# Latent attention's queries and keys turned by VectorE over device memory, with all such transfers issued by GpSimd

## The reference

```python
h = _rmsnorm(x, ln_g[l])
u = h @ w_in[l]                       # 2048 x 6232
y_a = _gla(...) * silu(g_a)           # gated linear attention
y_b = _ssd_mixer(...)                 # state space mixer
y_c = _mla(...) * silu(g_c)           # latent attention
y_d = _dilated_attention(...) * silu(g_d)
x = x + concatenate([y_a, y_b, y_c, y_d]) @ w_out[l]
```

```python
q = (_rmsnorm(c_q, q_norm_g) @ w_uq).reshape(Bsz, S, MLA_H, MLA_QK)
k = _rmsnorm(concatenate([k_nope, k_r]), k_head_g)
q = _rmsnorm(q, q_head_g)
q = concatenate([q[..., :128], _rope(q[..., 128:], positions)])
k = concatenate([k[..., :128], _rope(k[..., 128:], positions)])
return _causal_attention(q, k, v)
```

## Time and profile before

| | us |
|---|---|
| median of 3 runs | 814.8 (814.75 to 814.91) |
| the profiled execution, whole | 815.04 |
| its span, first to last instruction | 813.2 |
| TensorE busy | 806.8 (99%) |
| VectorE busy | 613.7 (75%) |
| ScalarE busy | 473.7 (58%) |
| GpSimd busy | 60.1 (7%) |
| SyncE's queue, share of the 16 transfer engines | 63.9% |

### The profile page before, as it was taken

The page is one execution under the profiler, slowest core; times in us unless marked ns, Lnnn a source line. Parts: engine busy times, 40 slices in busy tenths (PEclk is TensorE's granted clock), DMA queues, the critical chain, the costliest instruction groups (busy, mean ns, idle before and its releaser), DMA issues.

```text
span 813.2 us, 11261 instructions
## 1 busy us (share of the span) xinstructions
PE 806.8 (99%) x4164; PEld 684.3 (84%) x4164; DVE 613.7 (75%) x1092; ACT 473.7 (58%) x784; POOL 60.1 (7%) x64
## 2 busy tenths in 40 slices
PE   8999999999999999999999999999999999999998
PEld 5888887999887888888888888889998888888886
DVE  6678899877898766678964967979779977665452
ACT  6566544866965666433556465447687565664331
POOL 7100000110401000000000000003014010000000
PEclk9999999999999999999999999999999999999999
DMA  9956634586676967656576655355767677666553
GB/s 328 347 217 207 186 133 159 135 246 193 200 246 206 240 225 232 200 175 205 165 260 183 195 161 186 111 168 151 239 203 234 209 226 249 194 222 215 188 193 118
DMA packets 57687, 165.67 MB, mean 204 GB/s; under 512 B 6624, under 2 KB 14480, under 8 KB 57632
## 3 DMA queue, kind: packets, MB, share of 16 engines
q1 hardware_dynamic: 57120, 164.67, 63.9%
q10 hardware_dynamic: 320, 0.21, 0.1%
q0 software_dynamic: 192, 0.07, 0.1%
HBM read 155.47 MB, written 9.45 MB: 203 GB/s over the span
## 4 chain that ended last, share of the span: by engine, by line
PE 91%; DVE 6%; issue 2%; DMA 1%; ACT 0%; SPq 0%; DVEq 0%; ACTq 0%
PE gemm L705 27%; PE gemm L714 27%; PE gemm L706 26%; DVE arena L1345 3%; DVE w_lo L1384 2%; PE pairs L885 1%; PE pairs L855 1%; PE pairs L860 1%; PE pairs L856 1%; PE pairs L826 1%; PE pairs L771 1%; DVE arena L1473 1%; PE pairs L868 1%; PE pairs L899 1%; DMA u<-in_xT_dram 1%
## 5 line engine op out<-in xcount | busy, mean ns | idle before, releaser
L1384 DVE TENSOR_TENSOR w_lo<-raw,w_hi 128x1024 fp32r<-128x1024 f32 (+2 forms) x295 | 324.4, 1109 | 146.0 <-ACT w_hi L1019 144.3
L705 PE MATMUL gemm<-w_hi,a_hi 128*128 128x512 f32 (+1 forms) x1144 | 420.8, 373 | 0.3 <-ACT w_hi L1019 0.3
L706 PE MATMUL gemm<-w_hi,a_lo 128*128 128x512 f32 (+1 forms) x1144 | 414.3, 368 | 0.0
L1019 ACT ACTIVATE w_hi<-raw 128x1024 fp32r<-128x1024 f32 (+2 forms) x295 | 281.5, 968 | 214.1 <-PE gemm L714 137.0
L714 PE MATMUL gemm<-w_lo,a_hi 128*128 128x512 f32 (+1 forms) x1144 | 281.7, 368 | 0.2
L705 PEld LDWEIGHTS gemm<-w_hi,a_hi 128*128 128x128 f32 x1144 | 215.2, 188 | 36.4 <-issue 2.1
L706 PEld LDWEIGHTS gemm<-w_hi,a_lo 128*128 128x128 f32 x1144 | 215.2, 188 | 33.1
L714 PEld LDWEIGHTS gemm<-w_lo,a_hi 128*128 128x128 f32 x1144 | 203.2, 188 | 36.5 <-DVE w_lo L1384 1.9
L613 POOL TENSOR_TENSOR st<-st,powers 128x4 f32<-128x4 f32 (+2 forms) x8 | 10.1, 1263 | 429.5 <-ACT arena L1100 212.5
L1052 ACT ACTIVATE u<-gemm,st 128x512 f32<-128x512 f32 (+1 forms) x40 | 22.1, 603 | 15.8 <-PE gemm L714 15.8
L1221 ACT ACTIVATE arena<-arena,st 128x128 f32<-128x128 f32 (+1 forms) x32 | 13.1, 444 | 30.9 <-DVE st L1679 30.9
(11 more groups left out here) (201 smaller groups left out, 623.3 us busy)
## 6 DMA issues: line engine op xcount, KB each, us to landing
raw<-in_weights_dram SPq DMA_DIRECT2D x225, 512.0 KB, 4.3
raw<-in_weights_dram SPq DMA_DIRECT2D x64, 278.0 KB, 3.1
y_squares<-arena SPq DMA_DIRECT2D x6, 512.0 KB, 6.0
arena<-y_squares SPq DMA_DIRECT2D x24, 128.0 KB, 3.9
raw<-in_weights_dram SPq DMA_DIRECT2D x6, 384.0 KB, 4.4
x<-in_x_dram SPq DMA_DIRECT2D x4, 512.0 KB, 6.2
o<-ssd_rows SPq DMA_DIRECT2D x8, 256.0 KB, 5.4
param_rows<-in_params_dram SPq DMA_DIRECT2D x2, 904.0 KB, 7.0
```

The source lines that it names most:

```text
L705: pe.matmul(acc_t[t], a_hi[:, k, tok[t]], hi, start=k == 0, stop=False)
L706: pe.matmul(acc_t[t], a_lo[:, k, tok[t]], hi, start=False, stop=False)
L1019: A_(w_hi[:, g % SPLIT, 0:c], raw[:, g % RAW, 0:c], ACT.Copy).then_inc(hi_done, 1)
L1384: TT(w_lo[:, g % SPLIT, 0:c], raw[:, g % RAW, 0:c], w_hi[:, g % SPLIT, 0:c].bitcast(F32), ALU.subtract).then_inc(split_done, 1)
```

## The change

- The plain columns of latent attention's queries and keys are turned by squares. VectorE gets `mla q squares` at unit 80 and `mla k squares` at unit 85, two instructions of 128x512 each. TensorE's jobs `mla qT` and `mla kT` go; `mla rT` now waits for the rotation itself.
- The keys are used as they come back, in runs of 32, like those of the dilated attention. The queries are copied into order by ScalarE at unit 88 (`mla qT` is now the name of this copy); ScalarE's copy of the keys goes.
- `mla S 0` and `mla S 1` wait for `squares_in["mla k"]`. ScalarE's copy of the queries waits for `squares_in["mla q"]` and for VectorE's rotation.
- All squares' transfers leave SyncE and are issued by GpSimd, in one order with its `rsqrt` steps, each as soon as what it waits for is there.

```diff
-        "mla cT, ssd Y, mla qT, mla kT, mla rT, "
+        "mla cT, ssd Y, mla rT, "
...
+        SQUARES["mla q"] = fold[:, :], fold[:, :], 80
+        SQUARES["mla k"] = A(1024, 1024), A(1024, 1024), 85
...
-        mqT, mkT = two(A(0, 1024), 4), two(A(1024, 1024), 4)
+        mqT, mkT = two(A(0, 1024), 4), A(1024, 1024, "p (i h t a) -> p h t i a", i=4, h=4, t=T)
...
-                    for name, (_, _, at) in SQUARES.items():
-                        if n == at + 5:
-                            squares_out(l, name)
-                        if n == at + 7:
-                            squares_back(l, name)
...
+            def squares_out(l, name):
+                pool.wait_ge(*reached("dve", l)(f"{name} squares"))
+                pool.dma_start(squares_d[name], SQUARES[name][0]).then_inc(squares_out_done[name], 16)
+
+            def squares_back(l, name):
+                pool.wait_ge(squares_out_done[name], 16 * (l + 1))
+                away, to = squares_d[name].rearrange("(i b) (f c) -> f b i c", b=32, f=4), SQUARES[name][1]
+                for f in range(4):
+                    pool.dma_start(to[32 * f:32 * f + 32].rearrange("b (i c) -> b i c", i=4), away[f]).then_inc(squares_in[name], 16)
...
                 rsqrt("mla crs", crs, css)
+                squares_out(l, "ssd x")
+                squares_back(l, "ssd x")
                 rsqrt("mla rs 0", mrs[:, 0:8], mss[:, 0:8])
                 rsqrt("mla rs 1", mrs[:, 8:16], mss[:, 8:16])
+                squares_out(l, "mla q")
                 rsqrt("dil rs 0", drs[:, 0:8], dss[:, 0:8])
+                squares_back(l, "mla q")
                 rsqrt("dil rs 1", drs[:, 8:16], dss[:, 8:16])
+                squares_out(l, "ssd y")
+                squares_out(l, "mla k")
+                squares_back(l, "ssd y")
+                squares_back(l, "mla k")
+                squares_out(l, "dil q")
                 rsqrt("ssd rs", brs, bss)
+                squares_out(l, "dil k")
+                squares_back(l, "dil q")
+                squares_back(l, "dil k")
+                for name in ("y 1", "y 0", "y 2"):
+                    squares_out(l, name)
+                    squares_back(l, name)
...
-                    if rope:
-                        pe.wait_ge(*act("mla rT"))
-                    else:
-                        pe.wait_ge(*act("dil q"))
-                        pe.wait_ge(squares_in["dil k"], 16 * 4 * (l + 1))
+                    pe.wait_ge(*act("mla rT" if rope else "dil q"))
+                    pe.wait_ge(squares_in[f"{m} k"], 16 * 4 * (l + 1))
...
-                if n == slot("mla qT"):
-                    heads_T("mla qT", mqT)
-                if n == slot("mla kT"):
-                    heads_T("mla kT", mkT)
+                if n == 88:
+                    mla_qT()
...
+                    if n == SQUARES["mla q"][2]:
+                        head_squares("mla q", 0, "mla n 0 1", mqk)
...
+                    if n == SQUARES["mla k"][2]:
+                        head_squares("mla k", 1, "mla rope", mqk)
```

More of the change, by code:

```diff
@@ L247 @@
         "conv 0 3, conv 0 4, conv 0 5, ssd CB, mla cn, ssd x squares, ssd E 0, mla cT, ssd E 1, ssd M 0, ssd xdt, ssd M 1, "
-        "mla n 0 0, mla n 0 1, ssd yT, mla n 1 0, ssd y squares, mla n 1 1, mla rope products, mla rope, dil n 0 0, dil n 0 1, "
+        "mla n 0 0, mla n 0 1, ssd yT, mla q squares, mla n 1 0, ssd y squares, mla n 1 1, mla rope products, mla rope, mla k squares, dil n 0 0, dil n 0 1, "
         "dil n 1 0, dil n 1 1, dil rope 0 products, dil rope 0, dil rope 1 products, dil rope 1, gated 1, mla max 0, "
@@ L883, in scores @@
                         for t, (c0, c1, qs) in enumerate(parts):
-                            keys = k[:, h, 0:c1 - c0] if rope else k[:, h, 0:t + 1]
-                            last = pe.matmul(ps[:, r, c0:c1], q[:, h, qs], keys, start=c0 == 0, stop=not rope and c0 == P)
+                            last = pe.matmul(ps[:, r, c0:c1], q[:, h, qs], k[:, h, 0:t + 1], start=c0 == 0, stop=not rope and c0 == P)
                     if rope:
```

43 lines of the change are left out of this document (18 added, 25 removed), and 1 row of the table ORDER.

## The result

| | before | after |
|---|---|---|
| median of four runs each, us | 814.8 (814.75 to 814.91) | 827.2 (821.7 to 830.3) |
| ratio after to before | | 1.0138, interval 1.0118 to 1.0159 |
| profiled run, us | 815.04, span 813.2 | 825.13, span 823.1 |
| TensorE busy, us (matmuls) | 806.8 (4164) | 807.4 (4132) |
| time between the slowest and fastest run, us | 0.2 | 8.6 |

What follows compares the result with a forecast made beforehand. TensorE, busy 806.8 of 813.2 us, was taken as the bound. Lateness at mla S 0 of 0.8 and 0.4 us raised the profiled 815.04 to 816.2; the median, 0.2 lower, gave 816.0 us, range 813.8 to 821.5.

Steps and rivals of the forecast that it cites:

- What bounds the kernel, and what the jobs are worth: TensorE, busy 806.8 of 813.2 us, bounds the kernel; dropping four transposing jobs over both layers saves it 3.56 us.
- The place: At mla S 0: the wait for mla k's returned squares can set the time; mla rT's copy is a second gate.
- The size of the trip: mla k's squares out and back before mla S 0: 14.4 us, between 11.2 and 17.6, against 13.6 and 14.0 of room.
- The queue ahead of the trip: On GpSimd: only rsqrt steps and transfers needed much later stand behind a wait; no time was added for it.
- GpSimd starved: Rival: GpSimd's five transfer issues on the keys' path stretch by 0.39 us each, giving 820.0 us; chance 0.13.
- When the squares are ready: On VectorE after unit 85's low part: keys' squares done at 231.48 us in layer 0, 632.31 in layer 1.
- The price of being late: At mla S 0: lateness of 0.8 us in layer 0 and 0.4 in layer 1 adds 1.2 us to the time.
- What is cashed: At unit 93: VectorE's 2.44 us per layer of squares leave about 0.4 of the 3.56 us to be cashed.
- the relief of SP: Squares leave SP's queue, so weight loads no longer stand behind its waits for them; worth little, none taken.
- The page's rule on issuers: Transfers issued by GpSimd take 0.4 us longer per leg than by SyncE: trip 15.2 us, result 817.6 us.

Runs made afterwards that it cites:

- all trips together: Against the changed kernel: VectorE's squares of the keys at unit 82 instead of 85, their transfer out issued ahead of mla q's return; 827.42 us, ratio 1.0144.

## Why the prediction was wrong

- **What bounds the kernel, and what the jobs are worth: right.** TensorE bounds it, and the four jobs are worth 3.56 us, all of which the kernel without the squares' work cashed (1.79 and 1.82 us in its trace, span 809.4).
- **The place: right.** The trip of the keys ahead of mla S 0 sets the time, and the copy of mla rT is the second gate. The kernel that makes the trip without waiting for it is at 813.13 us. Between the two traces the sum is this: mla S 0 starts 4.0 us later than before in layer 0 and another 2.4 in layer 1, where I had 0.8 and 0.4; the lower clock takes 1.9, 1.0 and 0.6 us, where I had none. That makes the 9.9 us.
- **The size of the trip: the step that failed.** I added 5.6 + 1.8 + 7.0 = 14.4 us, with 17.6 at most. It was 20.2 us in layer 0 and 16.1 in layer 1, of which the next term has a part. The last landing was well sized (7.3, and 5.4 in layer 1). The way out was not in layer 0: 9.1 us instead of 5.6, outside of the 5.0 to 6.3 taken from the earlier trace rows. In layer 1 it took 6.1, inside of them, and in the other traces with the changed kernel's order it took 7.1 to 9.0. Those rows come from a crowded stretch, but of two transfers that started into it; here a transfer of 512 KB started together with ssd y's and beside the weights. I had mentioned that ssd y's trip moves into the same stretch and given it no term. A bound from rows holds for the company in which the rows were taken.
- **The queue ahead of the trip: a missing term.** I counted what stands behind GpSimd's waits and not what stands ahead of the keys: the two rsqrt steps of dil 1 and ssd y's issue, 1.8 us in layer 0 and 1.5 in layer 1, and in layer 1 another 1.4 us behind ssd y's four issues back; in layer 1 these 2.9 us are more than the whole 1.7 that the trip was over. The first of the two steps, 0.20 us at best in this trace, was held to 2.87 and 4.29 us. In both layers it ended 0.06 us behind the last of VectorE's tensor-tensor steps, just when the keys' squares had begun (227.82 behind 227.76, 637.36 behind 637.29). The second step takes its usual 1.65 us from there, and the squares only 1.22, so the keys' issue had to be late. This is the kin of my rival "GpSimd starved". Its mechanism did not occur (issues of the keys take 0.54 to 0.56 us), but a starved rsqrt step in front of them did. I had its rows in hand.
- **When the squares are ready: wrong, and in my favour.** I said 231.48 us in layer 0; it was 228.90, since VectorE came into the stretch 2.26 us earlier (211.00 against 213.26). This hid 2.6 us of the trip's error. In layer 1 it was 638.44, which is 632.5 without the 5.9 us by which layer 0 was late, and I had said 632.31.
- **The price of being late: wrong.** I took a microsecond of lateness as a microsecond of time. Idle TensorE also lost its clock: 6.70 us of wait cost 8.64, and 3.72 cost 4.69 and another 0.6 behind it.
- **What is cashed: mis-sized.** I let VectorE's stretch pin unit 93 and gave 0.03 us in layer 0 and 0.35 in layer 1. The kernel that makes the trip without waiting for it has unit 93 of layer 0 2.92 us earlier than the kernel before:

```profile
253.39 0.48 PE L718 MATMUL gemm<-w_hi,a_hi 128*128 128x512 f32 x1
```

  Of these, 1.25 us are there before the first job that went (unit 84 at 224.84 against 226.09): 0.65 from the first units of the program, where every trace differs, and 0.60 from SP's relief. The other 1.7 us are cashed from the jobs, of 1.78. In layer 1 only another 0.15 us are, as there TensorE waited 1.4 us for mla rT's copy. The kernel without the trip cashed 0.9 and 0.7 us. I had said that the relief of SP is worth none, because TensorE hardly waited for high parts. It is worth 0.6 us to TensorE, and 1.6 us to VectorE, as the run with GpSimd's issues alone shows. The stretch that I took as fixed starts that much earlier, and this pays for part of the 2.44 us of squares: in the changed kernel VectorE was ready for mla max 0 of layer 0 at 249.47, with both squares done, and before it began it at 249.56. In the trace of before it stood among the waits of VectorE for ScalarE's high part (the 2.7 us above), which I had not followed back to SP. The changed kernel lost this gain again at mla S 0.
- **The page's rule on issuers.** I had taken from the Trainium skill (DMA: Bandwidth & Descriptors, "Issuing engine by pattern" and the specifications) 0.4 us more per leg on GpSimd. The run with GpSimd's issues alone shows no such cost in time (ratio 0.9995), since those trips had room. A leg itself can be longer: ssd x's way out, which starts at the same place in both, took 4.19 and 4.11 us from SyncE in the kernel before and 4.63 and 4.79 from GpSimd in that run, near the page's difference; but ssd y's took 5.18 and 5.00 against 4.92 and 4.94. Neither size explains the keys' trip. No run here separates the two issuers on a trip that sets the end under equal load; with all squares on SyncE another queue, that of the weights, became the price.

What stays open: the spread. The same order gave waits of 6.7 and 3.7 us in one trace and 6.2 and 8.2 in that of the kernel with only the copy moved, and 8.6 us between the runs of the changed kernel. That two sets of transfers and the weights meet at slightly different moments fits this, but no run tried it.

## What to carry to other kernels

Give every transfer that an engine waits for its deadline in the profile, and write the order of the issuing queue by these deadlines; then add up for each what stands ahead of it in that queue and what else is in flight, not only its own legs. An order of the same work was worth 1.7% here, more than the change itself. And where TensorE bounds a kernel, a late operand can cost more than its lateness: read the granted clock behind the wait.

## What was not expected of the hardware

- After waits of 3.7 and 6.7 us TensorE went on at the lower level (windows at 0.69 and 0.59). After 6.7 us the eight products of mla S 0 took 2.90 instead of 1.48 us; after 3.7 they took 1.72, and the next eight 1.66 instead of 0.93. After waits of 0.5 to 2.0 us the first eight took 1.55 to 1.58 us. A wait of 2.45 us was already followed by 2.32 us for them and a window at 0.59 (ssd y wholly behind the keys, layer 1), the other waits of 3.6 to 8.2 us by 2.90 to 2.93. With the wait filled by products the clock stayed at 1.00.
- The landing of the keys' 512 KB out of the arena varied from 3.6 to 9.1 us with what lay beside it, all issued by GpSimd. That of weights of 512 KB issued between 224 and 236 us went from 5.7 us in the median (before) over 6.2 (the changed kernel) to 10.3 us (all trips together), while the share of the transfer engines from 222 to 245 us only went from 0.73 over 0.90 to 0.96.
- GpSimd's small tensor steps stretched to 2.9 and 4.3 us beside a busy VectorE, until 0.06 us behind the end of one of its tensor-tensor steps, while its issues of transfers in the same stretch stayed at 0.54 to 0.63 us.
